# A two-block network on one core: the order of VectorE's and ScalarE's filler work in the second recurrence

## The reference, cut to what matters

```python
def wkv_scan(r, v, decay, k, a_in, b_in, s0, reverse):
    def step(S, inp):
        rt, vt, wt, kt, at, bt = inp
        sa = jnp.einsum('bhij,bhj->bhi', S, at)
        S = S * wt[:, :, None, :] + sa[..., None] * bt[:, :, None, :] + vt[..., None] * kt[:, :, None, :]
        return S, jnp.einsum('bhij,bhj->bhi', S, rt)
...
decay = jnp.exp(-jnp.exp(w_log));  a = sigmoid(a0[d] + la_f @ a2[d]);  k_d = k * (1 + (a - 1) * k_a)
...
b_rw = y_rw.astype(dt) * jax.nn.silu(keep(rw_gate))
g_na, g_pool, g_rw = jnp.split(jax.nn.sigmoid(keep(merge_logits)), N_BRANCH, axis=-1)
merged = g_na * (b_na @ w_branch[0]) + g_pool * (b_pool @ w_branch[1]) + g_rw * (b_rw @ w_branch[2])
```

## Time and profile before

| | us |
|---|---|
| median of 3 runs | 3447.01 (3440.92 to 3453.52) |
| the profiled execution's own time | 3451.46 |
| its span | 3449.7 |
| TensorE (PE) busy | 3305.3 (96%) |
| VectorE (DVE) busy | 2156.9 (63%) |
| ScalarE (ACT) busy | 1569.9 (46%) |
| GpSimd (POOL) busy | 181.8 (5%) |

### The profile page before, as it was taken

How to read it: one execution, slowest core, us unless ns; L and a number is a source line. 1 busy time by engine, 2 the same in 40 slices (tenths; PEclk the granted TensorE clock), 3 DMA queues, 4 the chain that set the end, 5 groups by cost and what they waited for, 6 DMA issues and landing times.

```text
span 3449.7 us, 82807 instructions
## 1 busy us (share of the span) xinstructions
PE 3305.3 (96%) x37052; PEld 2997.4 (87%) x37052; DVE 2156.9 (63%) x3328; ACT 1569.9 (46%) x2415; POOL 181.8 (5%) x254
## 2 busy tenths in 40 slices
PE   7999999899889999999999999999999999999998
PEld 7988988899868888888888888988889999899987
DVE  8555755557557888886645444445556666667565
ACT  5433433445434444444434444433455555545443
POOL 0000000000000000000001110001211011110010
PEclk9999999999999999999999999999999999999999
DMA  5545554775435555555553333434433333343364
GB/s 200 212 159 183 208 183 158 271 262 179 176 117 180 184 184 188 190 184 208 183 183 136 118 133 130 147 129 165 161 124 125 128 128 129 119 136 132 116 232 149
DMA packets 94403, 571.60 MB, mean 166 GB/s; under 512 B 12689, under 2 KB 20913, under 8 KB 32097
## 3 DMA queue, kind: packets, MB, share of 16 engines
q1 hardware_dynamic: 80496, 511.85, 42.3%
q0 software_dynamic: 13552, 54.46, 4.7%
HBM read 535.98 MB, written 30.28 MB: 164 GB/s over the span
## 4 chain that ended last, share of the span: by engine, by line
PE 78%; DVE 9%; ACT 6%; issue 4%; DMA 3%; POOL 0%; SPq 0%; DVEq 0%; ACTq 0%; POOLq 0%
PE banks L292 15%; PE banks L293 7%; PE banks L1043 4%; PE banks L2170 3%; PE banks L316 3%; PE banks L317 3%; PE banks L318 3%; PE banks L1044 3%; PE banks L1045 3%; PE banks L279 3%; PE banks L280 3%; PE banks L281 3%; PE banks L2171 3%; PE banks L2172 3%; PE banks L2392 3%
## 5 line engine op out<-in xcount | busy, mean ns | idle before, releaser
L259 DVE TENSOR_TENSOR w_lo<-ring,w_hi 128x2048 fp32r<-128x2048 f32 x274 | 629.0, 2296 | 429.0 <-ACT w_hi L253 429.0
L253 ACT CAST w_hi<-ring 128x2048 fp32r<-128x2048 f32 x274 | 522.6, 1907 | 232.2 <-PE banks L281 94.4
L292 PE MATMUL banks<-x_two,w_hi 128*128 128x512 f32 x1408 | 499.2, 400 | 0.0
L293 PE MATMUL banks<-x_two,w_lo 128*128 128x256 f32 x1408 | 396.2, 281 | 0.0
L1043 PE MATMUL banks<-x_two,w_hi 128*128 128x256 f32 x1152 | 345.1, 300 | 5.0 <-DVE w_lo L1110 5.0
L2226 DVE TENSOR_TENSOR w_lo<-ring,w_hi 128x512 fp32r<-128x512 f32 x316 | 206.4, 686 | 200.2 <-ACT w_hi L2183 199.7
L1044 PE MATMUL banks<-x_two,w_hi 128*128 128x256 f32 x1152 | 328.8, 285 | 0.0
L1045 PE MATMUL banks<-x_two,w_lo 128*128 128x256 f32 x1152 | 328.4, 285 | 0.0
L292 PEld LDWEIGHTS banks<-x_two,w_hi 128*128 128x128 f32 x1408 | 265.3, 188 | 66.4
L2170 PE MATMUL banks<-XK,w_hi 128*128 128x256 f32 x1024 | 305.1, 298 | 0.3 <-issue 0.3
L2171 PE MATMUL banks<-XK,w_hi 128*128 128x256 f32 x1024 | 290.3, 284 | 0.0
(11 more groups left out here) (570 smaller groups left out, 7764.4 us busy)
## 6 DMA issues: line engine op xcount, KB each, us to landing
ring<-in_w_up SPq DMA_DIRECT2D x88, 1024.0 KB, 4.8
ring<-in_w_dil SPq DMA_DIRECT2D x72, 1024.0 KB, 5.0
mod_ring<-in_w_mod SPq DMA_DIRECT2D x48, 1024.0 KB, 8.2
ring<-in_w_logit SPq DMA_DIRECT2D x48, 1024.0 KB, 5.0
ring<-in_w_down SPq DMA_DIRECT2D x44, 1024.0 KB, 4.8
ring<-in_w_delta SPq DMA_DIRECT2D x32, 1024.0 KB, 4.8
ring<-in_w_out SPq DMA_DIRECT2D x32, 1024.0 KB, 4.8
ring<-in_w_na SPq DMA_DIRECT2D x32, 1024.0 KB, 4.8
```

What stands on the lines that cost most here:

```text
L253: nc.scalar.copy(w_hi[:, s, 0:w], ring[:, s, 0:w]).then_inc(S("panel_hi"), 4)
L259: nc.vector.tensor_tensor(w_lo[:, s, 0:w], ring[:, s, 0:w], w_hi[:, s, 0:w].bitcast(F32), ALU.subtract).then_inc(S("panel_split"), 4)
L292: nc.tensor.matmul(out_ap, hi, both, start=first_, stop=False)
L293: return nc.tensor.matmul(out_ap[:, 0, :], lo, both[:, 0, :], start=False, stop=last_)
```

## The change

VectorE takes two filler quarters fewer before the loop (6 in place of 8), so that within the loop its quarters are those that ScalarE cast one slot before. VectorE's `rates(b + 1)` moves from behind the quarters of slot F, masked(b, 1) and the output sum to directly behind `exclusive(b + 1)`. On ScalarE `key_scale(b + 1)` moves from behind the quarters of slot G to ahead of `turned(b, 1)`, and `exps(b + 1)` moves behind the quarters of slot G. The two hand-written orders follow. The whole diff:

```diff
--- before.py
+++ after.py
@@ -2335,14 +2335,14 @@
         act_order += [("u", s_, 0)] * st + [("xs", b), ("b2", b)] * inv
         act_order += [("rh", s_, 1)] * st + [("sigw", b + 1)] * nx
         act_order += [("u", s_, 1)] * st + [("x", b, 0)] * inv + [("sig", b + 1)] * nx + [("bhi", it_ - 1)] * back2
-        act_order += [("x", b, 1)] * inv + [("exps", b + 1), ("kd", b + 1)] * nx + [("tok", b)] * inv
+        act_order += [("kd", b + 1)] * nx + [("x", b, 1)] * inv + [("exps", b + 1)] * nx + [("tok", b)] * inv
         act_order += [("x", b, 2)] * inv + [("sq", it_ - 1)] * back
         dve_order += [("a", b), ("x0", b), ("aak", b)] * inv + [("bonus_in", it_)] * bonus
         dve_order += [("state", s_, 0)] * st + [("x2", b), ("a4", b), ("x3", b)] * inv
         dve_order += [("epi", it_ - 1)] * back2 + [("y", b, 0)] * inv
-        dve_order += [("xl", b, 0)] * inv + [("cum", b + 1)] * nx + [("state", s_, 1)] * first_
+        dve_order += [("xl", b, 0)] * inv + [("cum", b + 1), ("t", b + 1)] * nx + [("state", s_, 1)] * first_
         dve_order += [("s0", it_)] * back + [("blo", it_ - 1)] * back2
-        dve_order += [("y", b, 1)] * inv + [("yacc", s_)] * late + [("t", b + 1)] * nx
+        dve_order += [("y", b, 1)] * inv + [("yacc", s_)] * late
         dve_order += [("xl", b, 1)] * inv + [("bonus", it_)] * bonus
         dve_order += [("y", b, 2)] * inv + [("ar", b)] * (inv and tau >= 2) + [("cent", it_ - 1)] * back
         dve_order += [("tilde", b + 1)] * nx + [("xl", b, 2)] * inv + [("varx", it_ - 1)] * back
@@ -2751,17 +2751,17 @@
                 highs(it_ - 1)
             F(turns(i, "E"))
             F(turns(i, "F"))
+            if nx:
+                key_scale(b + 1)
 
             if inv:
                 turned(b, 1)
+            F(turns(i, "G"))
             if nx:
                 exps(b + 1)
-            F(turns(i, "G"))
 
             if not inv:
                 continue
-            if nx:
-                key_scale(b + 1)
             act.wait_ge(S("rw_mm"), mm("tok", b))
             nc.scalar.copy(TK[:, :, :, :, :].rearrange("p h k m c -> p h (k m c)"), pair(2, 0, 512)).then_inc(S("rw_act"), 1)
             aa.here("tok", b)
@@ -2928,7 +2928,7 @@
         F()
         k_tilde(0)
         a_tilde(0)
-        F(4)
+        F(2)
         dve.wait_ge(S("kv_stored"), 96 * WT)
         for i in range(NG + 1):
             b, s_ = i, i - 1
@@ -2991,6 +2991,7 @@
                 joined(b, 0)
             if nx:
                 exclusive(b + 1)
+                rates(b + 1)
             if st and s_ % 4 < 3:
                 advance(s_, 1)
             if back:
@@ -3013,8 +3014,6 @@
                         last = nc.vector.tensor_tensor(o, y, o, ALU.add)
                 last.then_inc(S("rw_dve"), 1)
                 vv.here("yacc", s_)
-            if nx:
-                rates(b + 1)
             F(turns(i, "G"))
             if inv and tau == 1:
                 r_shift(it_, 1)
```

## The result

The changed kernel took 3426.11 us (median of 6 runs, 3413.17 to 3431.84) beside 3445.51 for the kernel before on the same chip (6 runs): a ratio of 0.9933 (95% interval [0.991, 0.9957]), some 23 us less (15 to 31) where 15 were forecast. Two later comparisons of the same kernel gave 0.9930 [0.9914, 0.9946] and 0.9934 [0.9915, 0.9954].

A forecast was written before the change was run, and what follows sets the result against it. TensorE, busy 96% of the span, was taken as the bound, leaving only its idle time to gain. 18.9 us gone less 3.9 added gave 15.0 net: 3432.0 us against a 3447.01 median, range 3423 to 3447.

The forecast's parts named there:

- iX: TensorE's eight waits for VectorE's joined in the second recurrence, as in slot G: all 12.9 us go.
- XF: TensorE's two waits for VectorE's joined at level 2, slot I: all 1.5 us go.
- iBC: TensorE's six waits for ScalarE's turned: 2.8 of 3.8 us go, one 1.0 us wait stays in the first group.
- 1.7 us of clock: Slow clock (0.58 over four microseconds) behind TensorE's 3.69 us wait in slot G disappears: 1.7 us gained.
- charges for new waits: Times added within the loop for low-part splits, late panel loads and Silu's table load: 0.6, 1.5 and 0.9 us.
- rival A: Waits only move: later exponentials make TensorE wait 0.5 to 0.8 us in most groups; price 10 us, about 3442, chance 0.27.
- The added wait for w_lo: Slot G, four groups with the epilogue's low part queued: slot F's split about 0.2 us late, 0.6 us in all.
- The ring: Filler panels load one slot later; some long landings push slot G's exponentials in three groups: 1.5 us, bounds 0 to 56.
- AR behind Silu: Slot G of one group: Silu's table load precedes the exponentials, and TensorE's AR product waits for copy TK: 0.9 us.
- rival B: Panel loads, with one slot less, come late and make TensorE wait: 17 us slower, 3464; chance 0.08.
- The end: Last epilogue: VectorE's full split moves behind the variance, so the reciprocals start 0.9 us later.
- Rival C: Change does nothing: VectorE waits at once for something else and joined is no earlier; 3446, chance 0.05.

The follow-up runs named there:

- the lag alone: Kernel before, with only VectorE's filler quarters a slot behind and the old orders of exponentials, key scaling and rates: ratio 0.9948, stage 803.9 us.
- the orders alone: Changed kernel with VectorE's old lead of quarters before the loop, so only the orders differ from the kernel before: ratios 0.9939 and 0.9952, stage 809.9 and 809.2 us.
- the end variant: Changed kernel with the last epilogue's two whole-panel filler pieces (ScalarE's cast, VectorE's split) moved behind the chain: ratio 0.9946 to the kernel before.
- the catch-up: Changed kernel, with VectorE taking its two lagging quarters in the last group: ratios 0.9921 and 0.9923 to the kernel before, stage 799.8 and 798.2 us.
- the later loads: Changed kernel, with SP waiting for two more split quarters before loading a filler panel: ratio 1.010 to the kernel before, stage 857.6 us.
- the lag of three: Changed kernel, with VectorE three quarters behind ScalarE in place of two: ratio 1.0287 to the kernel before, stage 926.9 us.

## Why the prediction was right or wrong

The waits that go and the place were right: 15.0 us were forecast, and the stage gained 21.5 (the whole program 23 by the ratio). The step that failed is the sum. The prediction says that "all that an edit of the two others can bring is the idle time of TensorE", counts of that only the rows named iX, XF and iBC, and adds nothing for TensorE's busy time but the 1.7 us of clock; against it stand 3.0 us of charges for new waits, of which little came. In the mean of three profiles of each kernel (the first two rows from the stage's start to the mean):

| us of the stage | forecast | measured |
|---|---|---|
| idle time of TensorE less (17.2 less 3.0 of charges) | 14.2 | 17.9 (27.7 to 9.8) |
| busy time of TensorE less | 1.7 | 4.5 (779.8 to 775.3) |
| end later | 0.9 | 0.9 |
| sum | 15.0 | 21.5 |

Term by term:

- **iX and XF, 12.9 + 1.5: right.** Both are gone, and the lag alone takes them away.
- **iBC, 2.8 of 3.8: too little.** No wait was left, also in the first group: 1.0 more. After x1 the exponentials end 4.9 us later (2924.67 to 2929.55), beside 3.6 in the earlier trace rows, 1.3 of the 1.5 forecast. masked(b, 2) had to wait for TensorE (0.39 at 2932.54), not TensorE for it. The slack of that place was priced at 0.5 us and was 1.5: x2 is ready at 2933.86, and TensorE's level_b(b, 2) starts at 2935.40. So rival A falls, with more room than was argued. The figure that would have eaten a slack of 0.5, the Trainium skill's 2.7 us for a table load (ScalarE: Activation LUTs, "Table sets: the hidden batching unit"), is not what this trace has: 1.28 again, and the first exponential starts 0.02 us behind it.
- **The added wait for w_lo, 0.6: 0.5, but the agreement is luck.** That one slot of lead is enough was right (0, of bounds of 0 to 20), and three quarters show how near the edge is. But the one wait of 0.5 us is not before slot G in a group with the low part queued; it is behind level_b(b, 2) of the group that starts at 2939 us, and what is in front of it is the next point.
- **The ring, 1.5, and AR behind Silu, 0.9: 0.6 together, and it is the ring's.** The wait that was forecast for Silu is there, TensorE's AR product for the copy TK, but what stands in front of it is a late panel:

```profile
2965.22 0.38 ACT L2199 ACTIVATE RG<-banks 128x256 f32<-128x256 f32 x1
...
2971.54 0.39 ACT L2199 ACTIVATE RG<-banks 128x256 f32<-128x256 f32 x1
2974.53 0.62 ACT L2183 CAST w_hi<-ring 128x512 fp32r<-128x512 f32 x1 [2.61 <-DMA ring<-in_w_logit]
...
2978.04 0.99 ACT L2766 COPY TK<-banks 128x1024 f32<-128x1024 f32 x1
2978.24 0.69 DVE L2814 TENSOR_TENSOR BT<-BT,LdE 128x512 f32<-128x512 f32 x1 [4.05 <-ACT Lc L2653]
2979.09 0.69 PE L2601 MATMUL banks<-Lc,BT 64*64 64x64 f32 x32 [0.56 <-ACT TK L2766]
```

Silu's table load of the earlier trace rows is gone from this place: with the exponentials behind the casts, no load lies between this Silu and the one at 2965.22 (89 table loads in the program in place of 90, where the prediction had their number stay). The orders alone have the same Silu ahead of the exponentials, no wait for the ring, and no wait for TK. VectorE's b_tilde stands 4.05 us for the same exponentials, and from there its queue runs without a gap to the split that ends TensorE's 0.5 us wait for w_lo; the lag alone has no such wait. So the charge that came is the late load's, 1.0 us in all. In the two other profiles of the changed kernel the waits for TK are 1.3 and 0.6 us, again behind waits for the ring. A late load does reach TensorE, and where the prediction put it (the panel that begins in the middle of slot G), but rival B's price was far off: it is 1 to 2 us here, and 57.7 us of the stage with two quarters more. Where between the two the point lies was not measured.
- **Clock, 1.7: about 1.5.** The clock is 1.00 behind slot G, and the filler matmuls there are 1.5 us shorter. The prediction says that no other wait of the stage shows such a window, which misreads the trace: behind the 2.3 us wait at the stage's start the granted clock is 0.58, and after the change 0.57, in two of the three profiles of each kernel, so it cancels.

```profile
2475.90:2480.00 4.10, 4.07 (x104) 3.95 (x105) 3.45 (x6) 1.55 (x4) 1.77 (x3) 0.58 0.46 97
2462.00:2466.00 4.00, 4.00 (x104) 3.88 (x105) 2.14 (x4) 1.52 (x4) 1.66 (x3) 0.57 0.32 76
```

- **The end, 0.9: right** (13.3 to 14.2, in all profiles of both kernels). The b_lo wait itself grew from 4.11 to 6.45 us:

```profile
3262.74 0.58 PE L3152 MATMUL banks<-b_hi,w_hi 128*128 128x256 f32 x1 [6.45 <-DVE b_lo L2893]
```

Only 0.9 of this is the later chain. The wait was 4.1, 5.6 and 4.1 us in the three profiles before and 6.5, 5.0 and 6.5 after; the other 1.5 us come and go with a stretch of slow clock ahead of it, as in the first profile of the kernel before and not in its second:

```profile
3288.00:3292.00 4.00, 4.00 (x23) 4.00 (x22) 3.27 (x4) 0.84 (x2) 0.00 (x0) 0.57 0.54 135
3288.00:3292.00 4.00, 4.00 (x35) 4.00 (x35) 3.27 (x4) 0.75 (x2) 0.00 (x0) 1.00 0.44 131
```

Slower matmuls ahead make the wait shorter and the path no longer.
- **What the sum did not hold.** Of the 6.5 us, 1.0 is iBC, 1.7 the charges (3.0 counted; 1.0, 1.7 and 1.0 found) and 1.0 idle time that it named nowhere; in the last group alone 1.4, 0.5 and 1.1 us of idle time went to none. The other 2.8 are busy time. With the matmuls of the first profile of each kernel laid side by side, what is left of it beside the clock sits in pieces of 0.14 to 0.34 us, mostly next to a short idle time that went, and mostly in the level products (L2392). Why a matmul next to an idle time is booked longer stays open; ends of matmuls are modelled in the profile.
- Rival C is out: the cast waits went from 199.7 to 1.0.

## What to carry to other kernels

Where one engine prepares what a second one finishes for a third, let the second take pieces that the first finished a step ago: its in-order queue then hardly stands for them (199.7 us of waits became 1.0). How far behind it may run is set by the third engine's own lead, and here one quarter more decides (2 behind: 21.5 us gained; 3 behind: 105 us lost). Two cures of the same waits don't add (17.6 and 11.9 gave 21.5). Named waits are less than the gain (18.2 of 21.5), and the engine that a wait names can itself stand behind another: follow it one step further back. A change is to be measured over its stage, not over two spans, and over more than one profile.

## What was not expected of the hardware

The up projection (1065 to 1564 us of the span), untouched by every edit here, ran in the profiles at one of two paces. Before:

```profile
1100.00:1150.00 50.00, 50.00 (x285) 43.36 (x284) 41.61 (x64) 22.82 (x27) 0.00 (x0) 1.00 0.56 190
```

and after:

```profile
1100.00:1150.00 50.00, 50.00 (x291) 43.70 (x290) 42.54 (x64) 22.92 (x27) 0.00 (x0) 1.00 0.55 191
```

285 matmuls in 50 us, or 290 to 291, at the same granted clock of 1.00; over that stage some 499 us or 488 to 490. In 14 profiles of 8 programs each program always had the same pace, though only four were profiled more than once: the slow one the kernel before (three times), the lag alone, the end variant and the catch-up (twice), the fast one the changed kernel (three times), the orders alone (twice), the later loads and the lag of three. Runs without the profiler don't follow it: the catch-up took 3427.98 profiled and down to 3413.14 otherwise, and its median is no worse than the changed kernel's. What sets the pace I could not settle. It makes some 9 of the 35 us between the two spans; whether it has a part in the 19 to 28 us between the medians is not shown.
